# Layer-norm statistics by half-token pieces: column sums on four columns, rows by transposes

## The reference

```python
# between the blocks (N1): the end of the first block and the start of the second
h = h + gate * (p[i] @ w_ple_proj[i])
x = _rmsnorm(h, lnf_g)
x = layer_norm(x, ln_in_g, ln_in_b)          # mean and variance over 1024 features
# at the end (N2)
x = layer_norm(DEEPNORM_ALPHA * x + y, post_ln_g[l], post_ln_b[l])
```

## Time and profile before

| | us |
|---|---|
| median of the three runs | 1667.17 (1666.33 to 1669.31) |
| profiled execution, its time | 1670.05 |
| profiled execution, its span | 1668.3 |
| TensorE busy | 1622.8 (97%) |
| VectorE busy | 1155.8 (69%) |
| ScalarE busy | 623.9 (37%) |
| GpSimd busy | 708.8 (42%) |

### The profile page before, as it was taken

One profiled execution on the slowest core, in us unless ns is written; L12 is line 12 of the kernel. 1 busy time (PEld: TensorE's weight loads), 2 busy tenths in 40 slices (PEclk: granted clock), 3 DMA queues, 4 the chain that ended last, 5 costly groups with the idle time before them and its releaser, 6 DMA issues.

```text
span 1668.3 us, 21512 instructions
## 1 busy us (share of the span) xinstructions
PE 1622.8 (97%) x7830; PEld 1330.0 (80%) x7830; DVE 1155.8 (69%) x1702; ACT 623.9 (37%) x984; POOL 708.8 (42%) x389
## 2 busy tenths in 40 slices
PE   9999999999999999999999999999999999989997
PEld 6888787888877888888888778887878888878785
DVE  7231799972498777777767756886976993497466
ACT  6041334421164544444444222254562112269214
POOL 2443211145514223332226687752564555433452
PEclk9999999999999999999999999999999999999998
DMA  5511010123433443334449995322101111110112
GB/s 195 86 39 51 26 38 26 39 70 145 157 120 115 176 157 150 148 139 162 154 168 349 400 359 227 139 109 90 55 26 38 50 43 48 56 45 2 32 32 101
DMA packets 54455, 190.27 MB, mean 114 GB/s; under 512 B 5793, under 2 KB 7730, under 8 KB 53722
## 3 DMA queue, kind: packets, MB, share of 16 engines
q1 hardware_dynamic: 49250, 171.61, 28.4%
q10 hardware_dynamic: 5112, 17.44, 3.6%
HBM read 133.97 MB, written 55.05 MB: 113 GB/s over the span
## 4 chain that ended last, share of the span: by engine, by line
PE 54%; DVE 6%; DMA 3%; issue 2%; SPq 1%; POOL 1%; ACT 1%; ACTq 0%; POOLq 0%; DVEq 0%
PE G L795 15%; PE U L1042 10%; PE G L1042 10%; PE U L1080 4%; PE G L1080 4%; PE G L1116 4%; PE U L1207 1%; SPq L507 1%; PE U L1309 1%; PE G L1297 1%; DMA fraw<-in_weights 1%; PE G L1207 1%; DMA raw<-in_weights 1%; DMA hid_spill<-hst_last 1%; DVE h L2379 1%
## 5 line engine op out<-in xcount | busy, mean ns | idle before, releaser
L614 POOL TENSOR_SCALAR w_hi<-raw 128x1024 fp32r<-128x1024 f32 x49 | 146.7, 2994 | 284.4 <-PE G L795 211.7
L795 PE MATMUL G<-B_hi,w_hi 128*128 128x512 f32 x480 | 149.9, 393 | 3.0 <-DVE B_lo L2000 2.0
L795 PE MATMUL G<-B_lo,w_hi 128*128 128x512 f32 x480 | 147.9, 389 | 0.0
L795 PE MATMUL G<-B_hi,w_lo 128*128 128x512 f32 x480 | 147.8, 389 | 0.0
L795 PE MATMUL G<-A_hi,w_hi 128*128 128x512 f32 x448 | 144.6, 404 | 0.0
L657 POOL TENSOR_TENSOR S<-fraw 128x512 f32<-128x512 f32 x33 | 46.8, 1417 | 223.0 <-DVE ring_lo L2274 195.8
L795 PE MATMUL G<-A_lo,w_hi 128*128 128x512 f32 x448 | 138.9, 391 | 0.0
L795 PE MATMUL G<-A_hi,w_lo 128*128 128x512 f32 x448 | 138.6, 391 | 0.0
L616 POOL TENSOR_TENSOR w_lo<-raw,w_hi 128x1024 fp32r<-128x1024 f32 x49 | 131.2, 2677 | 4.1
L1042 PE MATMUL G<-X_lo,ring_hi 128*128 128x512 f32 x308 | 120.2, 390 | 2.2 <-DVE X_lo L2269 2.2
L1042 PE MATMUL G<-X_hi,ring_hi 128*128 128x512 f32 x308 | 120.1, 390 | 1.8 <-DVE ring_lo L2274 1.2
(11 more groups left out here) (407 smaller groups left out, 3847.0 us busy)
## 6 DMA issues: line engine op xcount, KB each, us to landing
raw<-in_weights SPq DMA_DIRECT2D x72, 512.0 KB, 3.5
hid_spill<-hst SPq DMA_DIRECT2D x72, 512.0 KB, 2.6
fraw<-in_weights SPq DMA_DIRECT2D x66, 512.0 KB, 4.4
Dc<-hid_spill SPq DMA_DIRECT2D x56, 512.0 KB, 12.3
Dc<-hid_spill ACTq DMA_DIRECT2D x14, 512.0 KB, 8.2
h<-in_x_t SPq DMA_DIRECT2D x8, 512.0 KB, 7.8
h_spill<-h SPq DMA_DIRECT2D x8, 512.0 KB, 6.5
pj_spill<-pj_out SPq DMA_DIRECT2D x8, 512.0 KB, 2.7
```

Source lines behind the costliest of these rows:

```text
L614: pool.tensor_scalar(hi, raw[:, u, :], 1.0, None, ALU.mult).then_inc(w_hi_done, 1)
L795: mm = pe.matmul(G[g][:, b * HT:(b + 1) * HT], w, x[:, k, b * HT:(b + 1) * HT], start=s0, stop=s1)
```

## The change

It touches both norms, both halves.

- The sums (`sums_by_block` in place of `sums_by_quarter`): the data is now the stationary operand (128 features by 128 tokens) and one column of ones is the moving one. Each matmul yields one column of 128 tokens on the partitions, so 512 tokens are four columns. The number of matmuls stays at four for each sum.
- The statistics work on four columns in place of 128.
- The rows (in `half_rows`): one column of `sm`, broadcast to 128, is transposed into 128 columns; four transposes give a row of 512 tokens. Each takes the place of one fp32 matmul.
- In N2's second half: six matmuls in place of ten stand ahead of the rows. On VectorE, `piece_summed(7)` is moved ahead of `normed(N2, 0, 4)`, and `normed(N2, 0, 5)` behind the factors of half 1. On ScalarE, three of the outputs are moved ahead of the last square; the output of k = 5 is moved behind the last root.

```diff
--- before.py
+++ after.py
@@ -262,7 +262,7 @@
         hg = at("hg", 120, [P, 2, T])
         acc2 = at("acc2", 40, [P, T])
         ones256 = at("ones256", 44, [P, P])
-        sm = at("sm", 45, [P, 2, 3, P])
+        sm = at("sm", 45, [P, 2, 3, 4])
 
         w3 = at("w3_hi", 0, [P, SLOT], F32R), at("w3_lo", 4, [P, SLOT], F32R)
         w4 = at("w4_hi", 48, [P, SLOT], F32R), at("w4_lo", 52, [P, SLOT], F32R)
@@ -390,8 +390,8 @@
         def sums_of_half(st, n, which):
 
             if st is N2 and n and which:
-                return G[0][:, 0:P]
-            return G[1][:, n * HT + which * P:n * HT + (which + 1) * P]
+                return G[0][:, 0:4]
+            return G[1][:, n * HT + which * 4:n * HT + (which + 1) * 4]
 
         early = [[G[1][:, 0:HT], G[1][:, HT:T]], [G[0][:, 0:HT], U[:, 2, :]], [G[0][:, HT:T], U[:, 1, :]], [U[:, 0, :], U[:, 3, :]]]
 
@@ -1119,11 +1119,11 @@
                             mm.then_inc(w_used, 1)
                 mm.then_inc(acc_done if n else pc_made, 1)
 
-            def sums_by_quarter(st, n, which, src, start=True, stop=True):
-
-                for g in range(4):
-                    mm = pe.matmul(sums_of_half(st, n, which)[g * QP:(g + 1) * QP, :], ones[:, 0:QP], src[:, g * P:(g + 1) * P],
-                                   start=start, stop=stop)
+            def sums_by_block(st, n, which, src, start=True, stop=True):
+
+                for c in range(4):
+                    mm = pe.matmul(sums_of_half(st, n, which)[:, c:c + 1], src[:, c * P:(c + 1) * P], ones[:, 0:1],
+                                   start=start and (c == 0 or stop), stop=stop, skip_group_check=not (start and stop))
                 return mm
 
             def half_sums(st, n, total, last=True):
@@ -1138,17 +1138,17 @@
                     pe.wait_ge(pc_read, st.made + 4)
                 pe.wait_ge(sum_done, st.sq + st.per * pieces)
                 pe.wait_ge(part_done, st.part + pieces)
-                sums_by_quarter(st, n, 0, acc[:, hs(n)], stop=last)
-                mm = sums_by_quarter(st, n, 1, total[:, hs(n)], stop=last)
+                sums_by_block(st, n, 0, acc[:, hs(n)], stop=last)
+                mm = sums_by_block(st, n, 1, total[:, hs(n)], stop=last)
                 if last:
                     mm.then_inc(stat_done, 1)
 
             def last_in_sums(st):
 
                 pe.wait_ge(d_done, st.d + len(PIECES))
-                sums_by_quarter(st, 1, 1, h[:, KT - 1, hs(1)], start=False)
+                sums_by_block(st, 1, 1, h[:, KT - 1, hs(1)], start=False)
                 pe.wait_ge(sq_done, st.sq + len(PIECES))
-                sums_by_quarter(st, 1, 0, sq[:, (KT - 1) % 2, hs(1)], start=False).then_inc(stat_done, 1)
+                sums_by_block(st, 1, 0, sq[:, (KT - 1) % 2, hs(1)], start=False).then_inc(stat_done, 1)
 
             def half_rows(st, n):
 
@@ -1157,9 +1157,8 @@
                 if st is N2 and n:
                     banks_of += [(G[0][:, 0:HT], 2), (G[1][:, 0:HT], 0)]
                 for dst, row in banks_of:
-                    for g in range(4):
-                        first = ident[:, g * QP:g * QP + 1].broadcast_to([P, P])
-                        mm = pe.matmul(dst[:, g * P:(g + 1) * P], first, sm[:, n, row, :], start=True, stop=True)
+                    for c in range(4):
+                        mm = pe.transpose(dst[:, c * P:(c + 1) * P], sm[:, n, row, c:c + 1].broadcast_to([P, P]), ident[:, :])
                     mm.then_inc(rows_done, 1)
 
             buf = [(w_hi[:, u, :], w_lo[:, u, :]) for u in range(2)]
@@ -1381,7 +1380,7 @@
                 piece(N2, j, (buf[1], buf[0], w3, w4)[j % 4], B_hi, B_lo, before=at_piece.get(j))
             last_in_sums(N2)
 
-            for _ in range(10):
+            for _ in range(6):
                 pe.matmul(G[1][:, 0:P], acc[:, 0:P], acc[:, 0:P], start=True, stop=True)
             half_rows(N2, 1)
 
@@ -1960,10 +1959,11 @@
             rows_kept(0)
             final(0), final(1), final(2)
             piece_square2(6)
-            for i in range(3, KT):
-                final(i)
+            final(3), final(4), final(5)
             piece_square2(7)
+            final(6)
             half_root(N2, 1, "ln_eps")
+            final(7)
             rows_kept(1)
             for i in range(KT, len(FINAL)):
                 final(i)
@@ -2826,10 +2826,11 @@
             piece_summed(5), piece_in(5)
             normed(N2, 0, 0, 1, 2, 3)
             piece_summed(6), piece_in(6)
-            normed(N2, 0, 4, 5)
             piece_summed(7)
+            normed(N2, 0, 4)
             half_variance(N2, 1)
             half_inverse(N2, 1), half_factors(N2, 1)
+            normed(N2, 0, 5)
             normed(N2, 1, *range(KT - 2))
```

## The result

The changed kernel takes 1670.80 us in the median of 22 runs, the kernel before 1668.66 us in 22 runs beside them. The ratio is 1.0013, with a 95% interval of 1.0007 to 1.0019: about 2.1 us slower. One execution of each kernel took far longer than the others (3492 and 2093 us); the ratio leaves them out. The forecast was +1.6 us, inside 0.2%. In absolute numbers it was 1668.8; 1.5 us of the distance to 1670.80 is that the kernel before itself has 1668.66 here and not 1667.17.

A forecast was written before the change was run, and what follows sets the result against it. TensorE's instruction stream (busy 97%) was taken as the bound, with a dependent chain after the last subtraction. +1.9 us before that point and -0.3 behind it made +1.6 on 1667.17: 1668.8 us, range 1663.3 to 1672.5.

The forecast's parts named there:

- A one-column pass: New sums on TensorE: each pass with one moving column taken at 0.106 us, bounds 0.036 and 0.190.
- Both rivals on this price: Sums' passes: as cheap as narrow ones (0.036, 1661.8 us, chance 0.17), or loads unhidden (0.190, 1675.5 us, chance 0.08).
- The loss of 1.13 for each sum: TensorE's stream: each half's sums insert 16 passes, 1.70 us in place of 0.57.
- The rows' gain of 0.87: TensorE's rows, each half: 8 transposes, 0.83 us, in place of 16 matmul passes, 1.70 us.
- N1: First norm: both halves lose +0.26 us each in TensorE's stream, sums +1.13 less rows 0.87.
- TensorE's 0.26: First norm's first half: +0.26 us, since TensorE's later finish of piece 6 takes up VectorE's gain.
- The hand-over of the slack: First norm's first half, piece 6: VectorE could read at 1204.5, TensorE finishes at 1205.7; nothing is won.
- Up to T: Stream until the end of the last piece's subtraction (L2817): 3 x 0.26 + 1.13 = +1.9 us.
- The tail: From the end of L2817 to the last output: 15.8 us against 16.08, -0.3; bounds -2.3 and +1.7.
- the clock as it fell before: Behind L2817: sums and eight filling passes at half rate, full clock back in the filling's last third.
- The clock in the stream: Rival: load-only stretches of sums count as idle; each half-clock stretch costs 1.65 us; one gives 1670.4; chance 0.20.
- The 1670.8 put beside it: Total in us if transposes don't count as busy, keeping the rows behind L2817 at half rate.

The follow-up runs named there:

- columns in N1: Kernel before with the change in the first norm alone, last norm as before: ratio 0.9997 to the kernel before, median 1667.48 against 1668.36 us.
- columns in N2: Kernel before with the change in the last norm alone, its order and six filling matmuls included: ratio 1.0017, median 1670.48 against 1668.36 us.
- ten filling: Changed kernel with ten filling matmuls again in place of six: ratio 1.0021 to the kernel before, median 1671.82 against 1668.36 us.
- sums off the stream: Changed kernel with seven eighths of the last sums moved from inside piece 7 to behind it: ratio 1.0002 to the kernel before, 1668.84 against 1668.70 us.
- wait filled: Changed kernel with six more filling matmuls between piece 7's end and the last sums: ratio 0.9998 to the kernel before, 1667.52 against 1668.70 us.

## Why the prediction was right, and where it was off

**A one-column pass** was put at 0.106 us, the rows' own; it is 0.111. The slope over columns in the earlier trace rows was enough. Both rivals on this price are refuted: 0.036 and 0.190. So is the floor of about 25 ns that the Trainium skill gives ("TensorE: Matmul & The Clock Gate", Part 1) as the bound here: with a full load ahead of each matmul it never comes to bear. The same page's section "LDWEIGHTS (loading the stationary operand)" says that a load's time goes by its columns alone, some 107 ns for 128. The pace of the passes, 111 ns, agrees within 4 ns; the record of one load is longer (192), and at the half clock the pace was 0.22.

**The loss of 1.13 for each sum** came out at 1.01: the present sums cost more than their 0.57. From the last matmul ahead of N2's first sums to the last of the piece, 24 steps of 0.227 later, the kernel before takes 0.84 us more than the steps and the changed one 1.85. The term that was mis-sized is the 0.57: it left out what the stream loses at its two edges (0.32 us to the first narrow pass and 0.34 behind the first matmul after it, in place of 0.23). **The rows' gain of 0.87** came out at 0.90. Together N2's first half cost +0.10, not +0.26.

**N1** was put at +0.52, and this is a step that failed, in two ways. From the last matmul ahead of the sums to the first behind the rows TensorE takes 8.44 us before and 8.50 after in the first half, 6.88 and 6.93 in the second: twice about +0.05, as small as the 0.10 of N2. And in the first half I followed TensorE's 0.26 through as a loss, after having shown myself that the tiles it waits for later come from VectorE's chain. That chain didn't move, and a lateness of TensorE would have gone into its wait of 1.5 us. The hand-over of the slack itself was right, down to the time at which VectorE could read (1205.7 foreseen, 1205.67 in the trace).

**Up to T** +1.9 was foreseen and +1.01 is in the profile: -0.17 stands already at the last matmul ahead of N2's first sums (1627.93 against 1628.10; ahead of N1 it was -0.16), N2's first half adds 0.10, and piece 7 with its last read adds 1.07, where 1.13 was foreseen.

**The tail** was put at -0.3, with bounds of -2.3 (all at full clock) and +1.7 (all at half). The profiled execution is +1.2, near the upper bound; the run at full clock is 13.73 against the 13.8 of the lower. The working of both ends was right and the choice between them was not: I let the clock return in the last third of the filling, as in the one execution that I had, and it didn't. Nor was it "the clock as it fell before". I put all 16 passes of the sums at half, from T on, and this window of the kernel before shows the fall at 1650.4, T + 0.7, with the sums of h already done at full:

```profile
1650.25:1650.50 0.25, 0.07 (x4) 0.07 (x8) 0.00 (x0) 0.13 (x1) 0.00 (x0) 0.76 1.03 393
```

With six passes at 0.106 and ten at 0.23 the sums end at T + 3.0, the factors at T + 4.6, the copy follows 2.15 later as in the lower bound, and the end is T + 15.0, or -1.1 (an estimate from the same rows). The forecast would then have been +0.8. From the medians, +2.1 less the 1.2 up to T, the tail costs about +0.9 on average. So too much before T and too little in the tail cancelled, and that the sum, +1.6, lies so near to +2.1 is luck in part.

**The clock in the stream** did not fall behind any of the sums in the profiled execution; N1 has its one half stretch during the waits for the normed tiles, as before (1216.25 to 1219.6, in the earlier trace rows 1216.9 to 1220.3). The profiles of five of the experiments (columns in N1, columns in N2, ten filling, sums off the stream, wait filled) have no half clock at all from 1180 to 1640, and the mean clock with columns in N1 alone is that of the kernel before. That rival is refuted as far as this goes. Its companion, the Trainium skill's rule that transposes don't count as busy (Part 4), isn't borne out: in the profile above the full clock came back at 1660.0 though only transposes had run since 1656.9 (with columns in N2 alone at 1658.2, only transposes since 1654.8). The 1670.8 put beside it was too much even so: rows at half make 12 transposes dearer by 0.104 each, 1.25 us, and 1670.8 is the whole tail at half. That came about, but it had begun before the last sums.

What stays open: whether the one-column passes by themselves bring the clock down, or only together with the wait. Filling the wait moved the fall behind the sums in one execution and raised the mean clock from 0.9938 to 0.9955. Against the wait as the whole cause speaks the run with the sums off the stream: there TensorE no longer waits, and the mean clock is 0.9942 all the same. Its profile, with none in the tail, is not its usual execution. The executions of a kernel differ here, and one profile of each is not enough to tell.

## What to carry to other kernels

A matmul against a column of ones is as dear as its weights: 128 columns of fp32 data as weights cost 0.11 us a pass here, whatever little moves, while narrow blocks of ones on four strips cost 0.036. Put such sums where TensorE waits anyhow: that took 1.87 us off the way to T here, where the change had put 1.2 on. Look first whether the reader is ready, though: with quarter sums it gained only 0.34 of 0.84, since VectorE was busy. When a chain behind the last dense work is followed step by step, price it at both clocks and look for what can stand in the wait ahead of it. And a lateness is only a loss if the next wait of that engine isn't longer.

## What the runs showed of the hardware that was not expected

- The half clock may last 10.2 us in one stretch (1649.75 to 1659.98) though TensorE is busy from 1650.78 on, with one-column matmuls to 1654.2 and 12 passes of filling to 1656.9. In the kernel before, the full clock was back at 1653.8, within the 20 passes of filling that began at 1651.0.
- The half clock may begin within a wait that is still short: at 1649.75 TensorE had been idle for 0.5 us of its 1.5.
- The same tail, in the same form, runs at full or in part at half clock from one execution to the next (last output at T + 15.19 and T + 16.08), so one profile of a kernel can be off by 0.9 us at this place. The tails with columns end anywhere from T + 13.73 to T + 17.26, but there the kernels differ ahead of T or in the filling.
